# Hybrid MLA and mLSTM step on one core: loops in place of written-out copies, and another split of x over its three tiles

## The chip, the cores and the metric

The kernel runs on one core of one Trainium2 chip. The metric is the device time of one execution in microseconds. The profile is that of one execution; its span runs from the first to the last instruction.

## The reference

One inference step of one layer, on 16 meta tokens, 256 prompt frames and 32 sample frames (304 tokens, `NT`). All projections are column blocks of one matrix `w_in` (4096 by 12,360); everything is float32.

```python
h = rmsnorm(x)                        # x: 304 tokens x 4096
cq, ckv, kpe, mq, mk, mv, mo, mi, mf, za, zb = split(h @ w_in)
q  = rmsnorm(cq) @ w_q_up             # 1536 -> 16 heads x (128 + 64)
kv = ckv_all @ w_kv_up                # 512 -> 16 heads x (128 + 128)
attn = softmax(mask(q k^T)) v         # block-causal over chunks of 64
ml_h = mlstm(mq, mk, mv, mi, mf)      # 4 heads, q and k 256 wide, v 512 wide
y = x + concat(attn * silu(za), sigmoid(mo) * rmsnorm(ml_h) * silu(zb)) @ w_out
```

## The kernel before

Each engine has its program of its own, and semaphores order them. A weight matrix goes through in units of 128 rows by 512 columns (384 or 512 in the attention stage). For each unit SyncE loads float32 rows into `raw` (4 slots of two units), ACT casts a unit to `whi` (L490, type fp32r), DVE subtracts and stores the remainder `wlo` (L857), and TensorE multiplies with both: the helper `mm3` does hi*hi (L1297), lo*hi (L1300) and hi*lo (L1301). `whi` and `wlo` have 4 slots (`HL_SLOTS`). ACT's and DVE's programs run 3 units ahead of TensorE's (`AHEAD`): the helper `steps` prepares unit k + 3 at step k, where the last three steps of a group prepare the first three units of the next. ACT waits for `unit_used` from TensorE, DVE for `hi_done` from ACT, TensorE for `lo_done` from DVE, and SyncE for `lo_done` too.

A group is 512 columns over all 32 units (`group` on TensorE): 32 x 12 matmuls into four PSUM banks, then four evictions, two by ACT and two by DVE. The stages are: x (below); `cq`, 3 groups; `ckv` and `narrow`; `bulk0` and seven `step` phases, each of which runs the projection of one pair of heads (12 units of `w_q_up`, 4 of `w_kv_up`) with the attention of the pair before placed between its units by hooks; `ml0qk`, `ml0v` and three `ml` phases, each with two groups and the mLSTM of one head in hooks; `gate0`, ten groups as five `gates` phases of two, `gate11`; `out0` and seven `out` groups of `w_out`. On TensorE, ACT and DVE all of this is written out by Python's `for`: the program is straight. SyncE and POOL have loops with a register (`Fori`) at the same places; SyncE's loop over the four mLSTM heads is at L416, and its loads are at L374.

The start: x is loaded in rows into three tiles `xt[0..2]` of 128 partitions by 4096, whose numbers of rows `X_TOK` gives: 112, 96, 96. All six DMAs are issued by ACT, first `xt[2]` (64 prompt rows, 32 sample rows), then `xt[0]` (16 meta rows, 96 prompt rows), then `xt[1]` in two halves of 2048 columns. ACT squares and sums each tile (L513, and L501 and L505 for the halves of `xt[1]`), DVE scales it (L870), and TensorE transposes it column block by column block (`x_tile`, L1323, three transposes for each of 32 blocks, after a wait at L1322 for every eighth block), interleaved with the first group of `cq`. SyncE waits for both halves of `xt[1]` (L383) before it issues the first weights. POOL loads the constants `con` and the gains `Grows`. Transposed, x is `xhi` and `xlo`, 304 columns.

With a Python number a wait's value is a constant; with a loop's variable it is computed in a register. Two places ask which it is: TensorE's `q_units` waits for `cq_lo` only where its pair is a Python number,

```python
                    pe.wait_ge(lo_done, U_PAIR + n * PAIR_UNITS + k + 1)
                    if isinstance(n, int):
                        pe.wait_ge(cq_lo, k + 1)
```

and ACT's first exponential skips a wait for pair 0.

Of the kernel before, what the change touches and what calls it, by code (L numbers as in the profile page):

```python
# [8 lines left out]
SEQ, DEC, PAST, N_META = 256, 32, 128, 16  # L9
# [29 lines left out]
TAIL = C_SAMPLE - 256  # L39

X_TOK = [(0, 112), (112, 96), (208, 96)]

WIDE = 72
# [16 lines left out]
XH = (slice(0, D_MODEL // 2), slice(D_MODEL // 2, D_MODEL))  # L62
# [105 lines left out]
def hymba_step(nc, x_prompt, x_sample, cache_ckv, cache_kpe, state_C, state_n, state_m, meta, norm_gain,  # L168
# [8 lines left out]
    with ctx:  # L177
        def keep(stack):
            return lambda name, shape, dt=f32: stack.enter_context(nc.sbuf_tensor(name, shape, dt))

        def sem(name):
            return ctx.enter_context(nc.semaphore(name))
# [27 lines left out]
        xt = [keep(p1)(f"xt{t}", [P, D_MODEL]) for t in range(3)]  # L210
# [113 lines left out]
        xrow_in = [sem(f"xrow{t}_in") for t in (0, "1_left", 2, "1_right")]  # L324
# [136 lines left out]
        def steps(n, now, after, hooks=lambda k: None):  # L461

            for k in range(n):
                if k + AHEAD < n:
                    now(k + AHEAD)
                elif after is not None:
                    after(k + AHEAD - n)
                hooks(k)
# [2 lines left out]
        @block.scalar  # L472
        def _(act):
            nc.scalar.preload_act_table_set("natural_log_exp_and_others")
            act.dma_start(xt[2][0:64, :], x_prompt[0, 192:256, :]).then_inc(xrow_in[2], 16)
            act.dma_start(xt[2][64:96, :], x_sample[0, :, :]).then_inc(xrow_in[2], 16)
            act.dma_start(xt[0][0:N_META, :], meta).then_inc(xrow_in[0], 16)
            act.dma_start(xt[0][N_META:112, :], x_prompt[0, 0:96, :]).then_inc(xrow_in[0], 16)
            for half, t in enumerate((1, 3)):
                act.dma_start(xt[1][0:96, XH[half]], x_prompt[0, 96:192, XH[half]]).then_inc(xrow_in[t], 16)  # L480
            junk = attnT[:, :, :].rearrange("p a b -> p (a b)")

            def unit(u, local, t, width=512):
# [12 lines left out]
            for done, t in enumerate(X_ORDER):  # L496
                n = X_TOK[t][1]
                if t == 1:
# [22 lines left out]
            def cq_units(i):  # L521
                return lambda k: unit(i * KT + k, k, landed(T_CQ, k, i * turns))
# [12 lines left out]
            def cq_evict(i):  # L535

                for ct in (0, 2):
                    act.wait_ge(full[ct], use("cq", ct, 0, i) + 1)
                    nc.scalar.copy(cqraw[:, ds(i * 4 + ct, 1), :], bank[ct][:, 0:NQ]).then_inc(free[ct], 1)
# [4 lines left out]
                    cq_units(0)(AHEAD - 1)  # L544
            steps(KT, cq_units(0), cq_units(1), lambda k: x_tile(k + 4) if k + 4 < KT else None)
            cq_evict(0)
            for i in range(1, 3):
                steps(KT, cq_units(i), cq_units(i + 1))
                cq_evict(i)

# [16 lines left out]
            def pair_units(n):  # L567
                def split(k):
                    unit(U_PAIR + n * PAIR_UNITS + k, k, landed(T_PAIR, k, n * pair_turns), 384 if k < KQ else 512)
                return split  # L570
# [36 lines left out]
            def v_evict(phase, i, n):  # L607

                for half, b in ((0, 1), (1, 2)):
                    act.wait_ge(full[b], use(phase, b, 1, i) + 1)  # L610
                    nc.scalar.copy(vt[:, 2 * half:2 * half + 2, :], bank[b][:, :].rearrange("p (a c) -> p a c", a=2))\  # L611
                      .then_inc(free[b], 1)
# [50 lines left out]
            def attention(phase, i, j):  # L663
                def hooks(k):
                    if k == 1:
                        k_rstd(phase, i, j)
                    if k == 6:
                        exps(phase, i, j, 0)
                    if k == 10:
                        pt_main(phase, i, j, 0)  # L670
                        exps(phase, i, j, 1)
                    if k == 12:
                        attn_evict(phase, i, j, 0)
                        pt_main(phase, i, j, 1)
                    if k == 13:
                        attn_evict(phase, i, j, 1)
                    if k == 15 and phase == "step":
                        q_rstd(phase, i, j + 1)
                return hooks
# [2 lines left out]
                return lambda k: unit(u + k, k, landed(before, k, extra, dmas))  # L682

            act.wait_ge(prob_zero, 1)
            for j in range(0, 6):
                steps(PAIR_UNITS, pair_units(j + 1), pair_units(j + 2), attention("step", j, j))
                v_evict("step", j, j + 1)
            steps(PAIR_UNITS, pair_units(7), big_units(U_ML, T_ML, 0, 2), attention("step", 6, 6))
# [85 lines left out]
                                      Cout[:, 0:2, :]).then_inc(Cp_out, 16)  # L774
                return hooks

            for h in range(0, 3):
                qk = big_units(U_ML + 2 * KT + h * (2 * KT), T_ML, (h + 1) * (3 * turns), 2)
                v = big_units(U_ML + 3 * KT + h * (2 * KT), T_ML, (h + 1) * (3 * turns) + 2 * turns)
                steps(KT, qk, v, mlstm("ml", h, h))  # L780
                qk_evict("ml", h, h + 1)

                steps(KT, v, big_units(U_ML + 4 * KT + h * (2 * KT), T_ML, (h + 2) * (3 * turns), 2))
                mv_evict("ml", 1, h, h + 1)
                act.wait_ge(Cp_out, 16 * h + 16)
# [12 lines left out]

            steps(KT, gate_units(0), gate_units(1), mlstm("gate0", 0, 3))
            gate("gate0", 0, 0)  # L800
            for g in range(0, 5):
                steps(KT, gate_units(2 * g + 1), gate_units(2 * g + 2))
                gate("gates", g, 2 * g + 1, 4)
                steps(KT, gate_units(2 * g + 2), gate_units(2 * g + 3))
                gate("gates", g, 2 * g + 2)
# [32 lines left out]
                    nc.scalar.copy(yT[:, ct, :], bank[ct][:, 0:NQ]).then_inc(free[ct], 1)  # L838

            y_evict("out0", 0, 0)  # L840
            for g in range(0, 6):
                steps(KT, out_units(g + 1), out_units(g + 2))
                y_evict("out", g, g + 1)
            steps(KT, out_units(7), None)
# [4 lines left out]
        def _(dve):  # L849
# [10 lines left out]
            for done, t in enumerate(X_ORDER):  # L860
                n = X_TOK[t][1]
                if done == 2:
# [27 lines left out]
                    cq_units(0)(k)  # L890
            steps(KT, cq_units(0), cq_units(1), lambda k: x_tile(k + 4) if k + 4 < KT else None)
            cq_evict(0)
            for i in range(1, 3):
                steps(KT, cq_units(i), cq_units(i + 1))
                cq_evict(i)

# [164 lines left out]
            def big_units(u):  # L1061
                return lambda k: unit(u + k, k)

            for j in range(0, 6):
                steps(PAIR_UNITS, pair_units(j + 1), pair_units(j + 2), attention("step", j, j))
                pair_end(j, j + 1)
            steps(PAIR_UNITS, pair_units(7), big_units(U_ML), attention("step", 6, 6))
# [148 lines left out]
                            ALU.mult, ALU.add).then_inc(free[7], 1)  # L1216
                return hooks

            for h in range(0, 3):
                qk = big_units(U_ML + 2 * KT + h * (2 * KT))  # L1220
                v = big_units(U_ML + 3 * KT + h * (2 * KT))
                steps(KT, qk, v, mlstm("ml", h, h))
                qk_evict("ml", h, h + 1)
                steps(KT, v, big_units(U_ML + 4 * KT + h * (2 * KT)))
                mv_evict("ml", 1, h, h + 1)
                dve.wait_ge(Cs_out, 16 * h + 16)
# [6 lines left out]

            steps(KT, big_units(U_GATE), big_units(U_GATE + KT), mlstm("gate0", 0, 3))
            silu("gate0", 0, 0)
            for g in range(0, 5):
                odd, even, after = (big_units(U_GATE + n * KT + g * (2 * KT)) for n in (1, 2, 3))
                steps(KT, odd, even)
                silu("gates", g, 2 * g + 1, 4)
                steps(KT, even, after)  # L1240
                silu("gates", g, 2 * g + 2)
# [35 lines left out]
                        add_rows("out", g, g)  # L1277
                return hooks

            for g in range(0, 6):  # L1280
                steps(KT, big_units(U_OUT + KT + g * KT), big_units(U_OUT + 2 * KT + g * KT), out_hooks(g))
                y_evict("out", g, g + 1)
                dve.wait_ge(y_out, g * 48 + 48)
# [8 lines left out]
        def _(pe):  # L1292
# [24 lines left out]
            def x_tile(k):  # L1317
                b = 4 + k % 4
                fill("x", b, k // 4)
                for t, (c0, n) in enumerate(X_TOK):  # L1320
                    if t == 0 and k % (KT // X_PARTS) == 0:
# [29 lines left out]
            for k in range(4):  # L1351
                x_tile(k)
            group(0, "cq", 0, 0, N_META, lambda k: x_tile(k + 4) if k + 4 < KT else None, x_ready=True)
            for i in range(1, 3):
                group(i * KT, "cq", 0, i, N_META)

            def cq_squares(k):
# [214 lines left out]
            pe.wait_ge(qn_zero, 1)  # L1572
            pe.wait_ge(prob_zero, 1)
            pe.wait_ge(pt_zero, 1)
            for j in range(0, 7):
                q_units(j + 1, "step", j, attention("step", j, j))
                kv_units(j + 1, "step", j, attention("step", j, j))
            group(U_ML, "ml0qk", 0, 0, 0, attention("ml0qk", 0, 7), queries=2)
# [138 lines left out]
                    pe.wait_ge(free[b], use("ml0v", b) + 1 + 2 * h)  # L1717

            pe.wait_ge(ml_zero, 6)
            for h in range(0, 3):  # L1720
                group(U_ML + 2 * KT + h * (2 * KT), "ml", 0, h, 0, mlstm("ml", h, h), queries=2)
                group(U_ML + 3 * KT + h * (2 * KT), "ml", 1, h, 0)
            group(U_GATE, "gate0", 0, 0, N_META, mlstm("gate0", 0, 3))

            for g in range(0, 5):
                group(U_GATE + KT + g * (2 * KT), "gates", 0, g, N_META, b0=4)
                group(U_GATE + 2 * KT + g * (2 * KT), "gates", 0, g, N_META)

# [16 lines left out]
                        ins = tr(bank[b][0:m, ct * P:ct * P + P], yT[:, ct, q0:q0 + m], ident)  # L1745
                    ins.then_inc(full[b], 1)

            for g in range(0, 7):
                group(U_OUT + KT + g * KT, "out", 0, g, N_META,
                      lambda k: y_rows("out", g) if k == 2 else None, a_hi=mhi, a_lo=mlo)  # L1750
            y_rows("outlast", 0)
# [234 lines left out]
```

## Time and profile before

| | |
|---|---|
| median of 3 runs | 2138.62 us (2138.28 to 2139.48) |
| the profiled execution | 2138.62 us |
| its span | 2137.0 us |
| TensorE busy, matmuls | 2089.4 us, 98% of the span |
| DVE, ACT, POOL busy | 49%, 42%, 10% |
| granted clock of TensorE, mean | 0.997 |

The profiled execution's time is 1.6 us longer than its span. PE is TensorE's matmul, PEld its weight load; a busy share is an average over all stages. A wait is listed under the engine that waited and the one that ended it.

### The profile page before, as it was taken

The page shows a single profiled execution, that of the slowest core. Times are in us where ns is not written, and L with a number is a line of the kernel's source. Part 1 is how long each engine was busy: PE and PEld are TensorE (multiplying, and loading weights), DVE is VectorE, ACT ScalarE, POOL GpSimd, SP SyncE. Part 2 cuts the span into 40 slices and gives each one's busy share as a digit, 9 for nine tenths or more (in the row PEclk, how much of TensorE's full clock was granted, in tenths as well). Part 3 has the DMA queues.
Part 4 walks back from the last instruction along what each step waited for, and adds up shares of the span by engine and source line. Part 5 has one row for each costly group of instructions (what it writes and reads, how often), then busy time and mean ns, then how long its engine had stood idle before and what let it go on. Part 6 is the DMA issues. An engine that isn't in the chain of part 4 may idle for free.

```text
span 2137.0 us, 38018 instructions
## 1 busy us (share of the span) xinstructions
PE 2089.4 (98%) x15062; PEld 2029.1 (95%) x15062; DVE 1047.2 (49%) x1868; ACT 891.4 (42%) x1751; POOL 218.5 (10%) x292
## 2 busy tenths in 40 slices
PE   4999999999999999999999999999999999999997
PEld 3999999999999899998999999999999999999997
DVE  4544565655544444443444444444445654444443
ACT  4543454545443333343333444444444543333332
POOL 1000123333200000000000000000001100000000
PEclk9999999999999999999999999999999999999999
DMA  7555433232455454554545555555555555555553
GB/s 195 155 164 159 117 121 94 89 104 80 119 149 163 119 163 122 153 145 118 178 123 155 167 167 164 165 167 167 165 163 166 164 181 183 180 180 183 186 188 105
DMA packets 189984, 321.92 MB, mean 151 GB/s; under 512 B 20524, under 2 KB 65680, under 8 KB 189424
## 3 DMA queue, kind: packets, MB, share of 16 engines
q1 hardware_dynamic: 182464, 296.92, 47.0%
q0 software_dynamic: 5488, 15.11, 2.1%
q10 hardware_dynamic: 1872, 7.60, 1.4%
q8 instruction: 119, 1.95, 0.4%
q14 instruction: 41, 0.34, 0.1%
HBM read 309.96 MB, written 9.62 MB: 150 GB/s over the span
## 4 chain that ended last, share of the span: by engine, by line
PE 97%; DMA 1%; DVE 0%; ACT 0%; issue 0%; ACTq 0%; POOL 0%; POOLq 0%; DVEq 0%; SPq 0%
PE bank L1297 29%; PE bank L1301 28%; PE bank L1300 28%; DMA xt<-in_x_prompt_dram 1%; PE bank L1693 1%; PE bank L1656 1%; PE bank L1545 1%; PE bank L1442 1%; PE bank L1443 1%; PE bank L1440 1%; PE bank L1457 1%; PE bank L1499 1%; PE bank L1510 1%; PE bank L1511 1%; PE bank L1745 0%; PE bank L1323 0%
## 5 line engine op out<-in xcount | busy, mean ns | idle before, releaser
L857 DVE TENSOR_TENSOR wlo<-raw,whi 128x512 fp32r<-128x512 f32 (+1 forms) x1256 | 824.3, 665 | 987.3 <-ACT whi L490 984.1
L490 ACT CAST whi<-raw 128x512 fp32r<-128x512 f32 (+1 forms) x1256 | 713.0, 577 | 1085.4 <-PE bank L1301 1043.9
L1297 PE MATMUL bank<-xhi,whi 128*128 128x288 f32 (+2 forms) x3104 | 936.7, 302 | 1.5 <-DVE wlo L857 1.2
L1301 PE MATMUL bank<-xhi,wlo 128*128 128x288 f32 (+2 forms) x3104 | 925.3, 298 | 0.0
L1300 PE MATMUL bank<-xlo,whi 128*128 128x288 f32 (+2 forms) x3104 | 924.2, 298 | 0.0
L1297 PEld LDWEIGHTS bank<-xhi,whi 128*128 128x128 f32 (+1 forms) x3104 | 585.0, 188 | 5.2 <-DVE wlo L857 1.5
L1300 PEld LDWEIGHTS bank<-xlo,whi 128*128 128x128 f32 (+1 forms) x3104 | 585.4, 189 | 1.9 <-issue 1.1
L1301 PEld LDWEIGHTS bank<-xhi,wlo 128*128 128x128 f32 (+1 forms) x3104 | 584.1, 188 | 0.0
L1297 PE MATMUL bank<-mhi,whi 128*128 128x288 f32 x1024 | 304.0, 297 | 0.0
L1300 PE MATMUL bank<-mlo,whi 128*128 128x288 f32 x1024 | 302.5, 295 | 0.0
L1301 PE MATMUL bank<-mhi,wlo 128*128 128x288 f32 x1024 | 302.5, 295 | 0.0
L1297 PEld LDWEIGHTS bank<-mhi,whi 128*128 128x128 f32 x1024 | 193.2, 189 | 0.9
L1300 PEld LDWEIGHTS bank<-mlo,whi 128*128 128x128 f32 x1024 | 193.1, 189 | 0.0
L1301 PEld LDWEIGHTS bank<-mhi,wlo 128*128 128x128 f32 x1024 | 192.7, 188 | 0.0
L1297 PE MATMUL bank<-cqhi,whi 128*128 128x288 f32 x288 | 92.1, 320 | 1.3 <-ACT vt L611 0.7
L1301 PE MATMUL bank<-cqhi,wlo 128*128 128x288 f32 x288 | 85.0, 295 | 0.0
L1300 PE MATMUL bank<-cqlo,whi 128*128 128x288 f32 x288 | 84.8, 295 | 0.0
L1297 PEld LDWEIGHTS bank<-cqhi,whi 128*128 128x128 f32 x288 | 54.4, 189 | 5.2 <-DVE wlo L857 1.1
L1300 PEld LDWEIGHTS bank<-cqlo,whi 128*128 128x128 f32 x288 | 54.6, 189 | 1.3 <-issue 1.2
L1301 PEld LDWEIGHTS bank<-cqhi,wlo 128*128 128x128 f32 x288 | 54.4, 189 | 0.0
L1943 POOL DMA_DIRECT2D out_dram<-ytok x24 | 12.9, 540 | 391.2 <-DVE ytok L1270 388.4
L1850 POOL TENSOR_SCALAR prob<-prob,pinv 128x144 f32<-128x144 f32 (+2 forms) x48 | 40.7, 862 | 116.6 <-DVE pinv L1028 116.6
(314 smaller groups left out, 1377.5 us busy)
## 6 DMA issues: line engine op xcount, KB each, us to landing
raw<-in_w_in_dram SPq DMA_DIRECT2D x316, 512.0 KB, 3.8
raw<-in_w_out_dram SPq DMA_DIRECT2D x128, 512.0 KB, 3.7
raw<-in_w_in_dram SPq DMA_DIRECT2D x140, 256.0 KB, 2.9
raw<-in_w_q_up_dram SPq DMA_DIRECT2D x48, 384.0 KB, 3.3
raw<-in_w_kv_up_dram SPq DMA_DIRECT2D x16, 512.0 KB, 3.7
xres<-in_x_prompt_dram POOLq DMA_DIRECT2D x16, 256.0 KB, 4.9
out_dram<-ytok POOLq DMA_DIRECT2D x16, 256.0 KB, 3.1
C<-in_state_C_dram POOLq DMA_DIRECT2D x4, 512.0 KB, 5.1
```

The source lines that it names most:

```text
L490: ins = nc.scalar.copy(hi, src)
L857: ins = tt(lo, src, hi.bitcast(f32), ALU.subtract)
L1297: ins = mm(out, w_hi, m_hi, start=start, stop=False, **kw)
L1300: mm(out, w_hi, m_lo, start=False, stop=False, **kw)
L1301: return mm(out, w_lo, m_hi, start=False, stop=stop, **kw)
L1440: mm(out, ckhi[:, k, cs], vcols(whi), start=k == 0 and half == 0, stop=False, skip_group_check=True)
L1442: mm(out, cklo[:, k, cs], vcols(whi), start=False, stop=False, skip_group_check=True)
L1443: ins = mm(out, ckhi[:, k, cs], vcols(wlo), start=False, stop=last, skip_group_check=True)
L1457: mm(bank[b][:, 0:NQ], ones if t < 2 else blockones, sq3[:, t, :], start=True, stop=True)\
L1499: mm(bank[b][:, 0:NKV], ones, sq2[:, t, :], start=True, stop=True).then_inc(full[b], 1)
L1510: mm(out, qn[:, h, q0:q0 + P], kn[:, h, 0:keys], start=True, stop=False)
L1850: ts_(prob[0:n, at:at + w], prob[0:n, at:at + w], pinv[0:n, t:t + 1], None, ALU.mult).then_inc(pn, 1)
```

## The change

`X_TOK` becomes 104, 100, 100, and the DMAs of x follow it. Ten `for` loops on ACT and DVE (five each) and five on TensorE become `Fori` loops with a register of the engine: `cq` groups 1 and 2, the `step` pairs (0 to 5 on ACT and DVE, 0 to 6 on TensorE), the `ml` heads 0 to 2, the `gates` phases 0 to 4, and the `out` groups (0 to 5 on ACT and DVE, 0 to 6 on TensorE). Their bodies are the same text. The diff, with one of each kind of loop in full and the rest cut:

```diff
-X_TOK = [(0, 112), (112, 96), (208, 96)]
+X_TOK = [(0, 104), (104, 100), (204, 100)]
...
-            act.dma_start(xt[2][0:64, :], x_prompt[0, 192:256, :]).then_inc(xrow_in[2], 16)
-            act.dma_start(xt[2][64:96, :], x_sample[0, :, :]).then_inc(xrow_in[2], 16)
+            act.dma_start(xt[2][0:68, :], x_prompt[0, 188:256, :]).then_inc(xrow_in[2], 16)
+            act.dma_start(xt[2][68:100, :], x_sample[0, :, :]).then_inc(xrow_in[2], 16)
             act.dma_start(xt[0][0:N_META, :], meta).then_inc(xrow_in[0], 16)
-            act.dma_start(xt[0][N_META:112, :], x_prompt[0, 0:96, :]).then_inc(xrow_in[0], 16)
+            act.dma_start(xt[0][N_META:104, :], x_prompt[0, 0:88, :]).then_inc(xrow_in[0], 16)
             for half, t in enumerate((1, 3)):
-                act.dma_start(xt[1][0:96, XH[half]], x_prompt[0, 96:192, XH[half]]).then_inc(xrow_in[t], 16)
+                act.dma_start(xt[1][0:100, XH[half]], x_prompt[0, 88:188, XH[half]]).then_inc(xrow_in[t], 16)
...
-            for i in range(1, 3):
+            with act.Fori(1, 3) as i:
                 steps(KT, cq_units(i), cq_units(i + 1))
                 cq_evict(i)
...
-            for j in range(0, 6):
+            with dve.Fori(0, 6) as j:
                 steps(PAIR_UNITS, pair_units(j + 1), pair_units(j + 2), attention("step", j, j))
                 pair_end(j, j + 1)
...
-            for h in range(0, 3):
+            with pe.Fori(0, 3) as h:
                 group(U_ML + 2 * KT + h * (2 * KT), "ml", 0, h, 0, mlstm("ml", h, h), queries=2)
                 group(U_ML + 3 * KT + h * (2 * KT), "ml", 1, h, 0)
...
-            for g in range(0, 5):
+            with pe.Fori(0, 5) as g:
                 group(U_GATE + KT + g * (2 * KT), "gates", 0, g, N_META, b0=4)
                 group(U_GATE + 2 * KT + g * (2 * KT), "gates", 0, g, N_META)
...
-            for g in range(0, 7):
+            with pe.Fori(0, 7) as g:
                 group(U_OUT + KT + g * KT, "out", 0, g, N_META,
                       lambda k: y_rows("out", g) if k == 2 else None, a_hi=mhi, a_lo=mlo)
```

## Rows read from the trace of the kernel before

**Rows 1.** The page: busy time, share and instructions of each engine.

```profile
PE 2089.4 (98%) x15062; PEld 2029.1 (95%) x15062; DVE 1047.2 (49%) x1868; ACT 891.4 (42%) x1751; POOL 218.5 (10%) x292
```

**Rows 2.** Stretches: length, busy us (count) by engine, clock, DMA share, GB/s.

```profile
0.00:34.40 34.40, 2.65 (x13) 2.17 (x13) 8.92 (x12) 16.81 (x21) 7.80 (x19) 1.00 0.89 212
2119.00:2137.00 18.00, 5.34 (x41) 4.82 (x40) 2.79 (x5) 0.80 (x2) 1.61 (x3) 0.81 0.09 33
```

**Rows 3.** Stretches of one cq group, step, ml, gates and out phase.

```profile
146.10:197.30 51.20, 51.20 (x387) 51.09 (x386) 22.95 (x35) 20.53 (x34) 0.00 (x0) 1.00 0.58 165
355.90:392.50 36.60, 36.60 (x250) 34.26 (x250) 21.25 (x55) 18.76 (x58) 12.00 (x14) 1.00 0.29 93
688.74:818.85 130.11, 130.11 (x877) 121.40 (x877) 55.91 (x103) 47.27 (x86) 2.94 (x4) 0.99 0.48 142
1290.00:1392.20 102.20, 102.20 (x772) 102.20 (x772) 49.93 (x73) 42.06 (x72) 8.02 (x8) 1.00 0.58 166
1760.79:1813.21 52.42, 52.42 (x398) 52.26 (x397) 24.58 (x37) 20.55 (x34) 3.23 (x6) 1.00 0.56 183
```

**Rows 4.** The chain of waits, its head: start us, us, what.

```profile
3.91 23.54 DMA xt<-in_x_prompt_dram
...
27.53 4.13 DMA raw<-in_w_in_dram
...
34.46 0.61 PE bank L1297
```

**Rows 5.** The stretch of that DMA of x.

```profile
3.91:27.45 23.54, 0.00 (x0) 0.00 (x0) 4.70 (x2) 10.31 (x10) 5.23 (x11) 1.00 1.00 223
```

**Rows 6.** DMA issues of x: count, KB each, median us to landing.

```profile
xt<-in_x_prompt_dram ACTq DMA_DIRECT2D x1, 1536.0 KB, 17.9
xt<-in_x_prompt_dram ACTq DMA_DIRECT2D x2, 768.0 KB, 21.8
xt<-in_x_prompt_dram ACTq DMA_DIRECT2D x1, 1024.0 KB, 7.8
```

**Rows 7.** SyncE's instructions by source line, 663.1:793.1, then 662.5:664 us.

```profile
L374 SPq FUSED_REGOPS  x48: 37/37/51, 665.6 to 792.3; - x48
L374 SPq MOVE raw<-in_w_in_dram x48: 29/29/29, 665.7 to 792.4; - x48
L374 SPq DMA_DIRECT2D raw<-in_w_in_dram x48: 372/373/986, 665.7 to 792.5; - x48
...
L373 SPq FUSED_REGOPS  x31: 46/51/51, 666.7 to 789.5; - x31
...
L416 SPq COMPARE_BRANCH  x1: 45/45/45, 662.9 to 662.9; - x1
L416 SPq FUSED_REGOPS  x1: 68/68/68, 663.2 to 663.2; - x1
```

**Rows 8.** TensorE by source line: the wait, and its transposes.

```profile
L1322 PEldq EVENT_SEMAPHORE  x1: 51/51/51, 42.9 to 42.9; - x1
...
L1323 PEld LDWEIGHTS bank<-con,xt x3: 142/142/142, 45.0 to 45.3; 96*128 96x128 f32 x2, 112*128 112x128 f32 x1
```

**Rows 9.** DMA queues (packets, MB, share of 16 engines) and small issues.

```profile
q8 instruction: 119, 1.95, 0.4%
q14 instruction: 41, 0.34, 0.1%
...
qpm<-in_barred_keys_dram POOLq DMA_DIRECT2D x2, 3.4 KB, 2.8
...
out_dram<-mrow POOLq DMA_DIRECT2D x2, 0.0 KB, 2.0
```

**Rows 10.** Timeline at two boundaries: start us, us, engine, line.

```profile
95.15 0.40 ACT L539 COPY attnT<-bank 128x288 f32<-128x288 f32 x1 [0.21 <-PE bank L1301]
...
95.28 0.81 DVE L885 COPY attnT<-bank 128x288 f32<-128x288 f32 x2
...
380.40 2.14 DVE L989 SCALAR_TENSOR_TENSOR qn<-qn,gsc,rsb 128x288 f32<-128x288 f32 x2
```

More of the change, by code:

```diff
@@ L684, in _ @@
             act.wait_ge(prob_zero, 1)
-            for j in range(0, 6):
+            with act.Fori(0, 6) as j:
                 steps(PAIR_UNITS, pair_units(j + 1), pair_units(j + 2), attention("step", j, j))
@@ L775, in mlstm @@
                 return hooks
-            for h in range(0, 3):
+            with act.Fori(0, 3) as h:
                 qk = big_units(U_ML + 2 * KT + h * (2 * KT), T_ML, (h + 1) * (3 * turns), 2)
@@ L800, in _ @@
             gate("gate0", 0, 0)
-            for g in range(0, 5):
+            with act.Fori(0, 5) as g:
                 steps(KT, gate_units(2 * g + 1), gate_units(2 * g + 2))
@@ L840, in _ @@
             y_evict("out0", 0, 0)
-            for g in range(0, 6):
+            with act.Fori(0, 6) as g:
                 steps(KT, out_units(g + 1), out_units(g + 2))
@@ L892, in _ @@
             cq_evict(0)
-            for i in range(1, 3):
+            with dve.Fori(1, 3) as i:
                 steps(KT, cq_units(i), cq_units(i + 1))
@@ L1062, in big_units @@
                 return lambda k: unit(u + k, k)
-            for j in range(0, 6):
+            with dve.Fori(0, 6) as j:
                 steps(PAIR_UNITS, pair_units(j + 1), pair_units(j + 2), attention("step", j, j))
@@ L1217, in mlstm @@
                 return hooks
-            for h in range(0, 3):
+            with dve.Fori(0, 3) as h:
                 qk = big_units(U_ML + 2 * KT + h * (2 * KT))
@@ L1235, in _ @@
             silu("gate0", 0, 0)
-            for g in range(0, 5):
+            with dve.Fori(0, 5) as g:
                 odd, even, after = (big_units(U_GATE + n * KT + g * (2 * KT)) for n in (1, 2, 3))
@@ L1278, in out_hooks @@
                 return hooks
-            for g in range(0, 6):
+            with dve.Fori(0, 6) as g:
                 steps(KT, big_units(U_OUT + KT + g * KT), big_units(U_OUT + 2 * KT + g * KT), out_hooks(g))
@@ L1353, in _ @@
             group(0, "cq", 0, 0, N_META, lambda k: x_tile(k + 4) if k + 4 < KT else None, x_ready=True)
-            for i in range(1, 3):
+            with pe.Fori(1, 3) as i:
                 group(i * KT, "cq", 0, i, N_META)
@@ L1574, in _ @@
             pe.wait_ge(pt_zero, 1)
-            for j in range(0, 7):
+            with pe.Fori(0, 7) as j:
                 q_units(j + 1, "step", j, attention("step", j, j))
@@ L1719, in _ @@
             pe.wait_ge(ml_zero, 6)
-            for h in range(0, 3):
+            with pe.Fori(0, 3) as h:
                 group(U_ML + 2 * KT + h * (2 * KT), "ml", 0, h, 0, mlstm("ml", h, h), queries=2)
@@ L1723, in _ @@
             group(U_GATE, "gate0", 0, 0, N_META, mlstm("gate0", 0, 3))
-            for g in range(0, 5):
+            with pe.Fori(0, 5) as g:
                 group(U_GATE + KT + g * (2 * KT), "gates", 0, g, N_META, b0=4)
```

## The prediction

> **What bounds the kernel now.** I read the busy times, then the table by stretches, then the head of the chain of waits. TensorE executes 15062 pairs of a weight load and a matmul and is busy 2089.4 of 2137.0 us [rows 1]. Its idle time is 47.6 us: 34.40 - 2.65 = 31.8 us ahead of the first real matmul and 18.00 - 5.34 = 12.7 us at the end [rows 2], so only some 3 us between. The reader is to see that after 34.4 us nothing but TensorE sets the pace, a pair every 0.13 us (51.20 / 387) [rows 3], and that work on another engine costs nothing while it is not late for it. Ahead of 34.4 us the chain is the loading of x: its transfers end at 3.91 + 23.54 = 27.45 us, then SyncE's first weights take 4.13 us, and TensorE starts at 34.46 us [rows 4]. In that stretch all 16 DMA engines are busy, share 1.00 at 223 GB/s [rows 5]. The profiled execution took 2138.62 us, which is also the median of the runs; its 1.6 us over the span stay. A difference under 0.2% (4.3 us) can't be told from none.
>
> **Part 1: the split of x.** No row is added: still 304 rows of 16 KB. The transposes keep their count (three a tile) and together their 304 columns; the squares and scalings of ACT and DVE run over the same 4096 elements, on 100 or 104 partitions: cost 0. What changes is how many rows one DMA carries. Before: 64, 32, 16, 96 and twice 96 half rows, with the sizes in [rows 6], all multiples of 16, so that each engine gets 4 + 2 + 1 + 6 + 3 + 3 = 19 rows. After: 68, 32, 16, 88, and twice 100 half rows. Sixteen engines can't share these equally, and no DMA of before from ACT or SyncE shows how such a one is dealt. The bounds:
>
> - as evenly as whole rows allow: the busiest engine gets 5 + 2 + 1 + 6 + 3.5 + 3.5 = 21, two more. At 23.54 / 19 = 1.24 us a row [rows 4] that is +2.5 us, and 0 if the others' lead is of use.
> - equal shares over as many engines as divide the rows: 68 over 4, 88 over 11, 100 over 10, each time from the same engine on. The first four get 17 + 2 + 1 + 8 + 5 + 5 = 38 rows, the last five 3. The pace then lies between 1.24 us and that of an uncrowded engine: 183 GB/s at share 0.56 [rows 3] is 20.4 GB/s an engine, 0.80 us a row. 38 rows take 30.4 to 47.1 us in place of 23.5: +6.9 to +23.6 us.
>
> I take the second deal, because equal shares are all that the transfers of before have. For the pace I take 0.90 us, near the uncrowded end, since eleven engines carry the bulk at first and four at the end: 38 x 0.90 - 23.5 = +10.7 us. The last half of xt[1] gates the last square and, through SyncE's wait, every weight transfer queued behind it; so all of it moves TensorE's start one for one, and nothing covers it. The Trainium skill (DMA: Bandwidth & Descriptors, "Why a DMA increments its semaphore by 16 and not by 1") states such a rule: the largest number of engines up to 16 that divides the slowest dimension, 10 for 100 partitions, and the lowest-numbered ones for DMAs from ACT or SP. By that rule 68 rows go to 4 engines; no row of before tests it.
>
> **Part 2: loops in place of written-out copies.** The same matmuls, casts and subtractions run. Added are a register instruction for each wait whose value depends on the loop's variable, and a branch an iteration. SyncE has such loops already: there a register instruction takes 0.04 to 0.07 us, and after a branch the next begins 0.3 us later [rows 7]. On TensorE one such wait a unit is 0.05 us against 12 x 0.13 = 1.6 us. Its sequencer has room: the wait at L1322 is over at 42.9 us, the transposes that it belongs to begin at 45.0 us [rows 8], so it works 2.1 us ahead. ACT and DVE are idle half the time [rows 1]. Cost 0; bounds -0.5, for the `cq_lo` waits that seven pairs lose, and +3, if 24 iterations lose 0.12 us each.
>
> The price is in fetching code. TensorE's queue fetched 119 packets of 16.4 KB, one for every 253 instructions, each taking 0.004 x 16 x 2137 / 119 = 1.15 us [rows 1, 9]; code that runs straight on is fetched ahead and shows no wait. A branch back may find its target gone. A fetch then costs between the 2.0 us of the smallest store and 2.8 + 1.15 = 4.0 us, a small load's landing and the packet [rows 9]; I take 3.0, and 0.3 for the branch. Of this 2.1 us are hidden by work already queued, which leaves 1.2 us each (0.2 to 2.2). TensorE branches back 1 + 6 + 2 + 4 + 6 = 19 times (cq, step, ml, gates, out). How many pay, no row says. The nearest is SyncE's loop over the heads: 3 x 48 + 31 + 3 = 178 instructions, more than one packet of its kind (8.3 KB, some 128), and it goes on after 0.3 us [rows 7, 9]; so more than the current packet is kept. TensorE's bodies fill 2 packets (step, 500 instructions), 3 (cq and out, some 780), 6 (gates, 1544) and 7 (ml, 1754 and its waits) [rows 3]. Between 0 and 19 I take those of gates and ml, 6 x 1.2 = +7.2 us: only these bodies are far from SyncE's in packets. The Trainium skill (Runtime: NRT & Kernel Launch, "Instruction fetch mechanics") is of two minds here: it gives TensorE room for 2048 instructions, by which at most ml would pay, and says that a taken branch out of a window of two pages waits for a fetch, by which nearly all 19 would. The trace has no loop on TensorE and settles neither.
>
> ACT and DVE branch back 17 times each. At the end of a column group of cq ACT's last eviction ends at 95.15 + 0.40 = 95.55 us and DVE's at 95.28 + 0.81 = 96.09 [rows 10]. TensorE then has three prepared units, 4.8 us from 95.8 on; the next needs 0.62 us of cast and 0.69 of subtraction before that. So ACT may lose 3.5 us and DVE 3.7 before TensorE waits: a fetch of 3.0 is hidden. Tightest is a pair's end: DVE is done at 380.40 + 2.14 = 382.54 [rows 10] and the fourth unit is due near 385.1, three units of 9 matmuls (3.6 us) and the squares of k (1.3) after 380.1; less the subtraction the cover is 1.9 us. DVE's body there is short: cost 0, or 5 x 1.4 = 7 us if it fetches. SyncE and POOL only follow.
>
> **The sum.** 2138.6 + 10.7 + 7.2 = **2156.5 us**.
>
> **Rivals.**
> 1. All 19 branches of TensorE fetch: 19 x 1.2 = 22.8; with part 1, 2172. For it: the shortest body already fills two packets, and one more is fetched ahead. Against: SyncE's loop.
> 2. No branch costs anything that shows: 2138.6 + 10.7 = 2149. For it: the 2.1 us ahead, and SyncE's loop. Against: bodies of six and seven packets.
> 3. The rows of x are dealt nearly evenly (+1.2): 2140 with free branches, 2147 with six that pay, 2163 with all. For it: each row can be a packet of its own. Against: that the sizes of before never needed it. The first of the three is no change.
> 4. Faster: the seven pairs of the step loop lose 12 waits each (84) on TensorE, at 0.05 us [rows 8] 4.3 us. It decides where TensorE's sequencer sets the pace there and part 1 costs nothing; 2134. Against it: TensorE is busy 36.60 of 36.60 us of a pair [rows 3].
> 5. As rival 1, with ACT and DVE late as well, or x at the slow end of its pace: 2185.
>
> **How the numbers follow.** Forecast (uneven deal, some branches pay) 0.36; rival 1 0.26; rival 2 0.20; rival 3 0.09, of it 0.05 within 0.2%; rival 4 0.02; rival 5 0.07. Faster 0.02, same 0.05, slower 0.93. The range leaves out rivals 4 and 5, most of rival 3 and the outer ends of the pace of x: 2145 to 2177.
>
> **What would show it.** Part 1: the DMA of x at the head of the chain lasts 34 us in place of 23.5, at a DMA share well under 1.00, and the first real matmul starts near 45 us. Part 2: TensorE is idle about a microsecond at the six boundaries of gates and ml and at none of step, cq and out; its fetched packets stay near 119 if bodies are fetched anew each time, and fall to some 50 if they are kept. Wrong would be: a first matmul before 38 us (the deal), or gaps at all 19 boundaries or at none. A gap that begins with a late subtraction on DVE, not in TensorE's own queue, would put the fault on the cover that I gave ACT and DVE.

## The result, and the profile after

The changed kernel takes 2194.84 us (median, 2193.24 to 2196.82), the kernel before 2139.05 (2138.28 to 2140.36): a ratio of 1.0261, 95% interval 1.0243 to 1.0279, so slower by 2.6%. The forecast was slower, by 18 us, in a range that ended at 2177; the loss is 56 us. The profiled execution took 2192.28 us, its span is 2190.7, 53.7 over that of before. One execution of the kernel before, beside the last experiments, took 2570 us at a mean granted clock of 0.75; no ratio counts it.

The page of the kernel after: busy time of the engines, the two queues that fetch code, and the costliest group of TensorE.

```profile
PE 2102.0 (96%) x15062; PEld 2040.3 (93%) x15062; DVE 1041.0 (48%) x1868; ACT 892.6 (41%) x1751; POOL 214.9 (10%) x292
...
q8 instruction: 104, 1.70, 0.3%
q14 instruction: 27, 0.21, 0.0%
...
L1297 PE MATMUL bank<-xhi,whi 128*128 128x288 f32 (+2 forms) x3104 | 942.0, 303 | 24.4 <-issue 21.8
```

TensorE executes the same 15062 pairs as in [rows 1], and is busy 12.6 us longer for them, so a part of the loss is a slower TensorE and not an idle one. Its idle time is 88.7 us in place of 47.6. The releaser "issue" means that the engine waited for nothing that the profile shows.

The start. The head of the chain of waits after (start us, us, what), TensorE's timeline at its first real matmul, and stretches of the loading of x (length, busy us by engine, clock, DMA share, GB/s):

```profile
3.39 42.29 DMA xt<-in_x_prompt_dram
45.75 4.74 DMA raw<-in_w_in_dram
```
```profile
53.28 0.61 PE L1297 MATMUL bank<-xhi,whi 128*128 128x288 f32 x1 [1.83 <-DVE wlo L857]
```
```profile
3.39:45.68 42.29, 0.39 (x1) 0.18 (x1) 4.80 (x4) 10.30 (x10) 5.74 (x12) 1.00 0.60 131
20.00:28.00 8.00, 0.00 (x0) 0.00 (x0) 0.00 (x0) 0.00 (x0) 0.00 (x0) 1.00 0.65 128
28.00:36.00 8.00, 0.00 (x0) 0.00 (x0) 0.63 (x1) 4.21 (x4) 0.00 (x0) 1.00 0.45 129
36.00:46.00 10.00, 0.39 (x1) 0.18 (x1) 4.28 (x4) 6.40 (x7) 0.00 (x0) 1.00 0.20 80
```

Against [rows 4, 5]: the transfers of x last 42.29 us, not 23.54, and TensorE starts at 53.28, not 34.46: 18.8 us. The share falls step by step, from 16 x 0.65 = 10 engines at work to 16 x 0.20 = 3: engines run out of rows one group after another, and a few work to the end. Equal shares give just that: four engines with 38 rows, six with 21, one with 11 and five with 3.

The loops. The idle time of TensorE by what ended it (total us, times, longest us), then the branches that close its five loops, each by its source line: cq, step, ml, gates, out (duration ns min/median/max, first and last start us):

```profile
PE bank L1315 <- DMA con<-in_shape_table_dram: 40.4, 1, 40.4
PE bank L1297 <- issue: 21.8, 6, 4.7
PE bank L1323 <- DVE xt L870: 8.4, 1, 8.4
```
```profile
L1354 PEldq COMPARE_BRANCH  x2: 83/167/251, 164.1 to 215.2; - x2
...
L1575 PEldq COMPARE_BRANCH  x7: 83/215/227, 360.9 to 581.0; - x7
...
L1720 PEldq COMPARE_BRANCH  x3: 83/4529/4772, 828.0 to 1094.3; - x3
...
L1725 PEldq COMPARE_BRANCH  x5: 76/3696/3793, 1271.3 to 1705.4; - x5
...
L1748 PEldq COMPARE_BRANCH  x7: 76/208/223, 1859.9 to 2174.1; - x7
```

Here the trace says it directly. The last branch of each loop falls through and takes 0.08 us. One that jumps back takes 0.2 us at cq, step and out, but 4.5 and 4.8 at ml and 3.3 to 3.8 at gates. TensorE stands still six times, as often as these two loops jump. First and last start give the iterations: ml (1094.3 - 828.0) / 2 = 133.15 us, gates (1705.4 - 1271.3) / 4 = 108.5, against 130.11 and 102.20 in [rows 3]; cq 51.1, step 36.7 and out 52.4 are as they were. That is 2 x 3.04 + 4 x 6.32 = 31.4 us. Another 1.0 us lies behind the late start: in its first 15.8 us of real matmuls TensorE executes 105, before 113, because those of 0.24 us go on for 5.8 us there and not for 3.0. With the 18.8 us, 51 of the 53.7 are placed; the rest is not.

A gates iteration is 6.3 us longer, but its gap is shorter: the four are 4.67, 3.85, 4.20 and 4.31 us, 4.3 in the mean. TensorE's timeline at the first, and stretches behind it:

```profile
1273.46 0.29 PE L1301 MATMUL bank<-xhi,wlo 128*128 128x288 f32 x1
1278.42 0.61 PE L1297 MATMUL bank<-xhi,whi 128*128 128x288 f32 x1 [4.67 <-issue]
1278.83 0.44 PE L1300 MATMUL bank<-xlo,whi 128*128 128x288 f32 x1
1279.07 0.44 PE L1301 MATMUL bank<-xhi,wlo 128*128 128x288 f32 x1
```
```profile
1278.42:1282.00 3.58, 3.58 (x15) 3.58 (x16) 0.69 (x1) 0.91 (x2) 0.00 (x0) 0.50 0.12 17
1282.00:1286.00 4.00, 4.00 (x24) 4.00 (x24) 1.38 (x2) 0.94 (x2) 0.00 (x0) 0.69 0.39 120
1286.00:1300.00 14.00, 14.00 (x108) 14.00 (x107) 5.95 (x9) 5.58 (x9) 0.00 (x0) 1.00 0.56 152
```

The branch starts at 1271.3, and the queued pairs cover it until 1273.75. After 4.67 us of idle the granted clock is 0.50 (1.2 GHz): 15 matmuls in 3.58 us, 0.24 us each and not 0.13, for some 6 us; behind the second and third gap it is some 3 us. From 1286 on it is back at 2.4 GHz. The remaining 2.1 us of the mean iteration lie there.

### The profile page after: what moved, and what is told of

It reads as the page before. It is cut to its first block, busy times and chain, and to the rows that moved or that the text cites. A ratio compares the mean times of both kernels' runs of the same rounds, so it can differ in the third digit from the quotient of the medians.

```text
span 2190.7 us, 41123 instructions
## 1 busy us (share of the span) xinstructions
PE 2102.0 (96%) x15062; PEld 2040.3 (93%) x15062; DVE 1041.0 (48%) x1868; ACT 892.6 (41%) x1751; POOL 214.9 (10%) x292
## 4 chain that ended last, share of the span: by engine, by line
PE 95%; DMA 2%; issue 1%; DVE 0%; ACT 0%; POOL 0%; ACTq 0%; DVEq 0%; POOLq 0%; SPq 0%
PE bank L1297 28%; PE bank L1300 28%; PE bank L1301 28%; DMA xt<-in_x_prompt_dram 2%; PE bank L1693 1%; PE bank L1656 1%; PE bank L1545 1%; PE bank L1443 1%; PE bank L1442 1%; PE bank L1440 1%; PE bank L1457 1%; PE bank L1499 1%; PE bank L1510 1%; PE bank L1511 1%; PE bank L1745 0%
## 5 line engine op out<-in xcount | busy, mean ns | idle before, releaser
L1297 PE MATMUL bank<-xhi,whi 128*128 128x288 f32 (+2 forms) x3104 | 942.0, 303 | 24.4 <-issue 21.8
```

What stands on the lines that cost most here:

```text
L1297: ins = mm(out, w_hi, m_hi, start=start, stop=False, **kw)
```

## The experiments

Theory of the split: rows are dealt in equal shares, over as many engines as divide them, and the first four engines get 38 of them. Rival: the number of DMAs, other tiles, or a nearly even deal. Theory of the loops: a jump back to code that TensorE no longer keeps waits for a fetch; rivals are late ACT or DVE, the branch itself, and what the bodies hold. "Before" is the kernel before, run on the same chip beside each set.

| kernel | us, median | ratio to before (95%) |
|---|---|---|
| loops only | 2176.94 | 1.0168 (1.0151 to 1.0185) |
| split only | 2158.49 | 1.0078 (1.0061 to 1.0095) |
| split, DMAs of 16 rows and remainders | 2146.93 | 1.0028 (1.0018 to 1.0038) |
| long bodies written out | 2140.79 | 0.9999 (0.9990 to 1.0009) |
| gates head at slot 0 | 2148.78 | 1.0037 (1.0024 to 1.0049) |
| hints at ml and gates | 2145.00 | 1.0018 (1.0009 to 1.0028) |
| out loop of two groups | 2177.04 | 1.0166 (1.0150 to 1.0183) |
| gates head at slot 200 | 2164.70 | 1.0113 (1.0093 to 1.0133) |
| the same with a hint | 2147.61 | 1.0037 (1.0025 to 1.0050) |
| both loops mended | 2141.64 | 1.0005 (0.9996 to 1.0014) |
| tiles 104, 104, 96 | 2148.97 | 1.0043 (1.0028 to 1.0057) |
| ten DMAs, one of 16 rows each time | 2142.91 | 1.0018 (1.0008 to 1.0028) |
| ten DMAs, equal cuts | 2146.36 | 1.0029 (1.0018 to 1.0040) |
| first 64 rows as 62 + 2 | 2163.70 | 1.0113 (1.0091 to 1.0135) |
| the change with both parts mended | 2146.56 | 1.0034 (1.0021 to 1.0047) |

Beside these, before had medians of 2140.3 to 2141.1 us, over a range of 2137.4 to 2143.0. Its profiled start is at the early end too: eight kernels here with its own six DMAs of x start real matmuls at 35.1 to 36.1 us, it at 34.46. Differences of a microsecond at the start, or of two in a median, are noise. The kernel with 62 + 2 rows was executed only twice.

### The parts by themselves

Loops only: the changed kernel with the old `X_TOK` and the old DMAs of x.

> The changed kernel with the split of x of the kernel before; all loops stay. If the two parts add up, the gaps that the profile after shows at the six back-branches of ml and gates stay (2.6 to 2.8 us at ml, 4.1 to 5.0 at gates, iterations longer by 2.9 and by 5 to 7 us), and the start is that of before, first matmul at 34.5 us: about 2139 + 6 + 25 = 2170 us. If the late start had caused the gaps (rival), they are gone and the time is 2139 to 2142.

Split only: the kernel before with the new ones.

> The kernel before with the new split of x alone. The uneven deal of rows over engines gives a DMA of x of some 42 us, a first matmul near 53 us and 2139 + 19 to 22 = 2158 to 2161 us. If the late start came from the loops (rival: code fetched on the same queues), it is 2139.

+35.8 us and +17.4 us: together 53.2, of 55.8 for the whole. The parts add up, and the late start caused no gap. The branches of the loops-only kernel at ml and gates:

```profile
L1720 PEldq COMPARE_BRANCH  x3: 76/4309/4697, 811.1 to 1078.3; - x3
...
L1725 PEldq COMPARE_BRANCH  x5: 76/3816/3886, 1255.3 to 1690.9; - x5
```

Iterations of 133.6 and 108.9 us: 7 + 27 = 34 us of its 35.8; I had expected 31.

### Which loops

Long bodies written out, in the loops-only kernel:

```diff
-            with pe.Fori(0, 3) as h:
+            for h in range(0, 3):
...
-            with pe.Fori(0, 5) as g:
+            for g in range(0, 5):
```

> The loops-only kernel with TensorE's two long loops (ml, gates) written out again; its cq, step and out loops stay, as do all loops of ACT and DVE. If only the long bodies pay, it takes the time of before, 2138 to 2141 us. If the loops of ACT and DVE have a part in the gaps (rival), some of the 31 us stays and shows as waits of TensorE for a subtraction at the ends of iterations of ml and gates: 2145 to 2170.

The time of before, with TensorE's 13 other back-branches and all those of ACT and DVE in place. So the whole loss of the loops comes from six branches.

### Length, or place

Out loop of two groups, in the loops-only kernel:

```diff
-            with pe.Fori(0, 7) as g:
-                group(U_OUT + KT + g * KT, "out", 0, g, N_META, ...
+            with pe.Fori(0, 3) as n:
+                for g in (2 * n, 2 * n + 1):
+                    group(U_OUT + KT + g * KT, "out", 0, g, N_META, ...
+            group(U_OUT + 7 * KT, "out", 0, 6, N_META, ...
```

> The loops-only kernel, with TensorE's out loop as 3 iterations of two column groups (some 1600 instructions a body, as gates has) and the seventh group written out; its loop of one group (some 780) showed no gap at 6 back-branches. If the length of the body decides, 2 gaps of 2.6 to 5 us appear at out and the time is 5 to 14 us over the loops-only kernel, 2175 to 2184. If it is what the bodies hold or where they lie (rival), none appears and it is 2170.

No new gap at out, and the time of the loops-only kernel (2177.04 and 2176.94). The body, 2 x 398 pairs [rows 3] and some 70 others, 1666 recorded instructions, is longer than that of gates and costs nothing, so length alone does not decide:

```profile
L1748 PEldq COMPARE_BRANCH  x3: 83/226/227, 1897.1 to 2106.6; - x3
```

The next kernel moves the gates body without changing it:

```diff
-            with pe.Fori(0, 5) as g:
+            with nc.Fori(0, 5, engines=OrderedEngineSet([pe.engine]), head_slot={pe.engine: 0}) as g:
```

> The loops-only kernel, with the head of TensorE's gates loop put at the start of a packet of code (254 to 256 instructions) by padding; nothing else changes. In the profile after, each back-branch of gates is followed by two packets in a row, some 3.2 us apart, at ml by one. Theory A (the head lies near the end of a packet, so the second packet is needed at once): one fetch is left to wait for, gaps fall from 4.1 to 5.0 us to 1.5 to 2.8 and with less slow clock after them, 2155 to 2163 us. Theory B (a body of that length is kept if it spans no packet more than needed): no gaps at gates at all, only those of ml stay, near 2145. Theory C (neither matters): as the loops-only kernel, 2170.

Theory B held: the gaps of gates are gone. And with `head_slot={pe.engine: 200}`:

> The loops-only kernel with the head of TensorE's gates loop put at slot 200 of a packet of 256 instructions. The body has some 1610 instructions: from slot 0 it ends in the seventh packet, from 200 in the eighth (200 + 1610 = 1810, over 1792). If the body is kept as long as it lies in seven packets, the gaps of 4 to 5 us at four back-branches are back, 27 us of them: 2170 to 2177 us. If the padding alone mended them in the kernel with the head at slot 0 (rival), none: 2149.

They are back, though shorter. TensorE's branches at gates (a placed loop has one more, the jump into its head), its waits on "issue" and its packets of code, first with the head at slot 0 (the idle left is that of ml):

```profile
L1726 PEldq COMPARE_BRANCH  x6: 76/212/295, 1154.0 to 1663.9; - x6
```
```profile
PE bank L1298 <- issue: 6.3, 3, 2.9
```
```profile
q8 instruction: 68, 1.11, 0.2%
```

and at slot 200:

```profile
L1726 PEldq COMPARE_BRANCH  x6: 76/4723/5198, 1149.9 to 1678.8; - x6
```
```profile
PE bank L1298 <- issue: 16.9, 8, 3.0
```
```profile
q8 instruction: 105, 1.72, 0.4%
```

The gates body has 772 pairs [rows 3] and 65 others, 1609 instructions recorded from one closing branch to the next. A packet holds 256: TensorE's 30538 recorded instructions of the kernel before came in 119, 256.6 each. From slot 0 the body ends in the seventh packet, from 200 in the eighth. In seven it is kept, in eight fetched anew at each turn, 37 packets more. The rival that padding alone mends is out.

The total was 5 us under my expectation because the gaps are 2.4 to 3.0 us here, and 3.9 to 4.7 in the changed kernel, although the branch is longer here (4.6 to 5.2 us, against 3.3 to 3.8). The trace of the changed kernel shows what follows its first branch at gates, by source line:

```profile
L1725 PEldq FUSED_REGOPS  x1: 50/50/50, 1275.2 to 1275.2; - x1
L1311 PEldq ALU_OP  x1: 36/36/36, 1275.3 to 1275.3; - x1
```

Two instructions of the body run, and the third, a weight load, starts at 1278.42, 3.1 us later. The fetches of two packets start at 1272.6 and 1275.8 us. So it is at all eight waiting branches of gates in this kernel and the loops-only one: a stop of 2.8 to 3.4 us after two instructions. The head therefore lies two instructions before the end of its packet, at slot 254, and a second fetch is waited for at once. From there the body ends at 254 + 1609 = 1863, over 7 x 256 = 1792: eight packets.

From this head the recorded instructions can be counted to the others of the loops-only kernel and of the one with the out loop of two groups. The ml head is 1855 + 1000 instructions earlier, at slot 215; TensorE does run 256 - 215 = 41 instructions behind a branch at ml and then waits 0.7 and 0.9 us more. The head of the out loop of two groups is 1609 + 1573 later, at slot 108, and its body ends at 108 + 1666 = 1774. That is in the seventh packet, so its 0.2 us follow the same rule.

### The hint

```profile
L1726 PEldq COMPARE_BRANCH  x6: 88/228/292, 1149.6 to 1659.5; - x6
```
```profile
q8 instruction: 69, 1.13, 0.2%
```

Branches of 0.2 us and 36 packets fewer, and none fetched from 1237 to 1661 us: with the hint a body of eight packets is kept. It does not only order the target early. From this I made a rule, seven packets without and eight with a hint, and from it what mends ml, which has more than seven packets of code from any slot. Both loops mended has the gates head at slot 0, and `head_slot={pe.engine: 0}, hint_back_edge=True` on ml:

> The loops-only kernel with the gates head at slot 0 without a hint, and the ml head at slot 0 with a hint. The runs so far fit this rule: without a hint a body is kept if it lies in seven packets (gates from slot 0, the loops of up to 1674 instructions), with one if it lies in eight (gates from slot 200, after which no packet was fetched until the loop ended). The ml body has some 1817 instructions, 25 over seven packets, so it lies in eight from slot 0 and in nine from most other slots. If the rule holds, ml is kept too: no gap at any of the 19 back-branches, no packet fetched for TensorE between 830 and 1050 us, and 2140 to 2143 us, as the kernel with these two loops written out. If the hint only orders the target early (rival), ml's code is fetched anew each time and what it showed with a hint elsewhere stays, 1.6 and 2.3 us an iteration: 2144 to 2146 us.

```profile
L1721 PEldq COMPARE_BRANCH  x4: 80/234/310, 680.6 to 1070.3; - x4
...
L1726 PEldq COMPARE_BRANCH  x6: 76/212/401, 1143.8 to 1653.7; - x6
```
```profile
q8 instruction: 49, 0.80, 0.2%
```

The rule held. No branch of the 19 waits, 49 packets are fetched, and the time can't be told from that of before. One count in my expectation was wrong: the body has 1855 recorded instructions, 1856 with the hint, and touches nine packets only from slots over 192, not from most. In the kernel with hints its head lay in such a slot: again 41 instructions run behind the branch before TensorE waits, so it is slot 215, 215 + 1856 = 2071 is over 8 x 256, and ml paid in spite of its hint (branches of 2.9 and 3.1 us). Slot 0 without a hint was not tried at ml.

### The deal of x

Split with DMAs of a multiple of 16 rows and a remainder:

```diff
-            act.dma_start(xt[2][0:68, :], x_prompt[0, 188:256, :]).then_inc(xrow_in[2], 16)
+            act.dma_start(xt[2][0:64, :], x_prompt[0, 188:252, :]).then_inc(xrow_in[2], 16)
+            act.dma_start(xt[2][64:68, :], x_prompt[0, 252:256, :]).then_inc(xrow_in[2], 16)
...
-                act.dma_start(xt[1][0:100, XH[half]], x_prompt[0, 88:188, XH[half]]).then_inc(xrow_in[t], 16)
+                act.dma_start(xt[1][0:96, XH[half]], x_prompt[0, 88:184, XH[half]]).then_inc(xrow_in[t], 16)
+                act.dma_start(xt[1][96:100, XH[half]], x_prompt[0, 184:188, XH[half]]).then_inc(xrow_in[t], 16)
```

> As the one before it, but each DMA of 68, 88 and 100 rows is cut into one of a multiple of 16 rows (64, 80, 96) and a rest of 4 or 8; the same tiles of 104, 100 and 100 rows. If the deal of rows over engines is the cause, most of the lateness goes: the busiest engines have 4 + 1 + 2 + 1 + 5 + 1 + 3.5 + 3.5 = 21 rows, 2 more than before, so about 2.5 us late, 2141 us. If the tiles' sizes or the count of rows on partitions were the cause (rival), it stays at 2158 to 2161.

Two thirds are back (from +17.4 to +5.8 us), where I expected nearly all. Tiles of 104, 104 and 96 rows, with DMAs of 88 and twice 104 rows as the odd ones:

> The kernel before with x split into tiles of 104, 104 and 96 rows: DMAs of 64, 32, 16, 88 rows and twice 104 half rows. If equal shares over as many engines as divide the rows decide, 64 rows go to 16 engines, 88 to 11, 104 to 13, and the busiest get 4 + 2 + 1 + 8 + 4 + 4 = 23 rows, against 38 in the split of the change and 19 before. At the 1.12 us a row of the split-only kernel (42.44 / 38) to the 1.24 of before that is a DMA of x of 26 to 28.5 us, 2 to 5 us late, 2143 to 2146 us. If any size that isn't a multiple of 16 costs alike (rival), the two halves and the 88 rows bring most of the 17 us of the split-only kernel: 2150 to 2158. If the 7 us that the split with remainders kept come from tiles of other sizes, about 2147.

Between the two theories: +8.5 us, 3 over the top of what the deal gives and one under the rival's foot. Only the next one is sharp. The first DMA of before, 64 rows, as 62 and 2:

```diff
-            act.dma_start(xt[2][0:64, :], x_prompt[0, 192:256, :]).then_inc(xrow_in[2], 16)
+            act.dma_start(xt[2][0:62, :], x_prompt[0, 192:254, :]).then_inc(xrow_in[2], 16)
+            act.dma_start(xt[2][62:64, :], x_prompt[0, 254:256, :]).then_inc(xrow_in[2], 16)
```

> The kernel before, its tiles unchanged, with the first DMA of x, 64 rows, cut into one of 62 rows and one of 2. By equal shares over as many engines as divide the rows, 62 go to 2 engines, 31 each, and these have 31 + 1 + 2 + 1 + 6 + 3 + 3 = 47 rows. With 0.66 us for each of the 28 rows over 19 (79 GB/s at share 0.20 in the stretch 36 to 46 us of the split-only kernel is 24.7 GB/s an engine) the DMA ends 18 us late, with its mean of 1.12 us a row for all 47 it lasts 53 us, 29 late: 2159 to 2170 us. If rows are dealt singly to whichever engine is next (rival), it lasts 24 to 25 us and the time is 2141 to 2143.

The head of its chain, and the stretch to the end of x:

```profile
2.71 42.77 DMA xt<-in_x_prompt_dram
```
```profile
27.45:45.48 18.03, 0.39 (x1) 0.18 (x1) 0.28 (x1) 4.20 (x4) 0.00 (x0) 1.00 0.12 49
```

A share of 0.12 is 1.9 of 16 engines: two work, alone, for 18 us. 49 / 1.92 = 25.5 GB/s each, 0.64 us a row, and 28 rows more than the other engines' 19 take 28 x 0.64 = 18 us. The equal shares are shown, and with them the 38 rows of the change. The load ends 18.0 us later than before and the first matmul starts 23.7 later (58.18 us), because `xt[2]`, whose square ACT takes first, is now the tile that comes last.

What stayed open is why the split with remainders kept 5.8 us. Ten DMAs with the old tiles, 16 rows split off each time (48 + 16, 80 + 16, 80 + 16 twice):

> The kernel before, its tiles of 112, 96 and 96 rows unchanged, with the DMAs of 64, 96 and twice 96 rows each cut into a multiple of 16 and one of 16 rows (48 + 16, 80 + 16, 80 + 16 twice): ten DMAs for x, as in the split with remainders, which stayed 5.8 us over before. If the number of DMAs costs that, this kernel takes about 2147 too, with a DMA of x of some 30 us. If the remainders of 4 and 8 rows, which reach 4 or 8 engines, do (rival), each engine has its 19 rows, the DMA stays at 23.5 to 24.5 us and the time at 2141.

and ten with equal cuts (32 + 32, 48 + 48, 48 + 48 twice):

> As the kernel with ten DMAs for x, which ended them at 32.4 us against 27.5 to 27.8 with six, at share 1.00 but 185 GB/s against 223; here the cuts are equal (32 + 32, 48 + 48, and 48 + 48 twice), so no DMA gives an engine a single row. If the number of DMAs slows the engines, they end near 32.4 again and the time is 2142 to 2144. If small ones of one row an engine do (rival), they end by 29 us: 2141.

The stretch of [rows 5] with remainders, with 16 rows split off, with equal cuts, and with tiles of 104, 104 and 96 rows:

```profile
3.91:27.45 23.54, 0.00 (x0) 0.00 (x0) 2.35 (x1) 4.46 (x5) 5.23 (x11) 1.00 1.01 163
```
```profile
3.91:27.45 23.54, 0.00 (x0) 0.00 (x0) 2.35 (x1) 7.88 (x6) 5.23 (x11) 1.00 1.00 185
```
```profile
3.91:27.45 23.54, 0.00 (x0) 0.00 (x0) 2.35 (x1) 7.28 (x5) 5.26 (x11) 1.00 1.02 169
```
```profile
3.91:27.45 23.54, 0.00 (x0) 0.00 (x0) 2.35 (x1) 6.45 (x5) 5.23 (x11) 1.00 0.91 174
```

With ten DMAs the engines are as full as before, share 1.00 to 1.02, and move 163 to 185 GB/s in place of 223. Equal cuts are no better (2146.36 to 2142.91), so small pieces are not the reason. Nor is it the number of DMAs alone: the last row has six, and there a busy engine moves 174 / (16 x 0.91) = 12.0 GB/s, against 13.9 before and 11.6 and 10.4 with ten evenly dealt. Its DMA of x lasts 31.06 us for the 23 rows of the busiest engine, 1.35 us a row, which is where its 3 us over the deal come from. In this stretch every other deal than that of before had slower engines; why, these runs don't tell.

Last, the whole change with the DMAs of the split with remainders and the loops as in the kernel with both loops mended:

> The whole change with both faults mended: the split into 104, 100 and 100 rows with the DMAs in multiples of 16 and remainders, and all loops, with the gates head at slot 0 and the ml head at slot 0 with a hint. If the parts are independent, its time is that of the split with remainders and free loops, 2146 to 2148 us, with no gap at any back-branch. If the later start or more DMAs disturb the fetches (rival), gaps are back and it takes 2150 or more.

2146.56 us, no branch that waits: all 6 us left are those of the split. The two parts are independent within the noise.

## Why the prediction was wrong

**Direction and mechanisms** were right, that gates pays in part by luck: x dealt in equal shares, 38 rows on four engines; a pay at the six back-branches of ml and gates, none at the other 13; ACT and DVE never late, and SyncE's wait passing the late x on to the first weights. Two terms were sized wrong, and both sizes were too small; these are the steps that failed.

**The term "38 x 0.90 - 23.5 = +10.7"** measured 18.8 us (first matmul) and 17.4 (split only). It is inside its bounds of 6.9 to 23.6. What failed is the pace "near the uncrowded end, since eleven engines carry the bulk at first and four at the end". The trace gives 42.29 / 38 = 1.11 us a row. In the stretch 20 to 28 us only 0.65 of the engines were busy, and yet each moved 128 / (16 x 0.65) = 12.3 GB/s, under the 13.9 of a full one in [rows 5]; the uncrowded pace came only after 36 us (80 / 3.2 = 25 GB/s, 0.66 us a row). Fewer busy engines did not make the others faster while ten of them worked, and in that stretch of the loading no kernel with a changed deal kept the pace of before. For bounds so far apart the middle, 1.0 us, would have given 14.5.

**The term "6 x 1.2 = +7.2"** measured 31.4 us, 5.2 a branch, outside its bound of 2.2. The six gaps are 21.8 us of it. It had three faults:

- "A fetch then costs between 2.0 and 4.0 us; I take 3.0". The waiting branch takes 3.3 to 5.2 us over the kernels without hints. Those of ml in the changed kernel, 4.5 and 4.8, leave gaps of 2.3 and 2.5 where 2.2 was the bound. A small load's landing and a packet were no upper bound.
- One fetch was counted a branch. At gates of the changed kernel two are waited for, and the idle time is 3.9 to 4.7 us; with the head at slot 200 and one fetch it is 2.4 to 3.0.
- The clock was left out. Behind the gaps of gates TensorE runs at 0.50 for 3 to 6 us, 2.1 us more an iteration. A stall of the engine that bounds a kernel costs more than itself.

**Which bodies pay.** "Only these bodies are far from SyncE's in packets" picked the right six, but length was not the measure. What decides is the number of packets that the body touches, seven or eight, and that hangs on where its head falls: the same gates body costs nothing at slot 0, and the longer out body nothing at slot 108. The counts of six and seven packets took pairs alone; with the other instructions and the heads at slots 254 and 215 it is eight and nine. ml would pay at any slot without a hint by this rule, but gates only from the 72 slots over 183 of 256. There the layout decided, and the prediction had no reason for it; from the other slots rival 2's free branches would have been true of gates.

**The marks given.** DMA of x 34 us: it took 42.3. First matmul near 45: 53.3. Idle about 1 us at six boundaries: at those six, 2.3 to 4.7. Packets near 119 if fetched anew, some 50 if kept: 104, and 49 once all are kept. Rival 5, 2185, came nearest in time, for reasons that did not hold.

**The pages.** The Trainium skill (DMA: Bandwidth & Descriptors, "Why a DMA increments its semaphore by 16 and not by 1") gives the largest number of engines up to 16 that divides the rows, from the lowest on. The runs agree: two engines for 62 rows, +23 us. The Trainium skill (Runtime: NRT & Kernel Launch, "Instruction fetch mechanics") gives TensorE room for 2048 instructions, and the runs agree, with the qualification that the eighth packet is there only with a hint. Its other statement, that a branch out of a window of two pages waits, differs from the measurement: the out body of two groups, some 1670 instructions, jumps back in 0.2 us. The measurement decides.

## What to carry to other kernels

Before a written-out body becomes a loop, count its instructions in packets of code and ask where the head will lie: the duration of the closing branch in the trace (0.2 us, or 3 to 5) tells in one row whether the body is kept, and a hint or another slot can mend it without a change of the work. Count the rows of a DMA by their divisors, not their sum: 4 rows more than 64 cost 13 more on the busiest engine. Where bounds of a price lie three times apart, and the engine that would wait is the one that bounds the kernel, take the middle or above, and add what the slow clock takes after the stall.

## What was not expected of the hardware

- TensorE keeps a body that touches seven packets (1792 instructions), and eight with a hint at its top: 105 fetched packets against 69 for the same code at the same slot, but for the hint.
- A branch back to code that is gone takes 3.3 to 5.2 us without a hint. A head two instructions before the end of its packet costs a second wait of some 3 us. Behind gaps of 3.9 to 4.7 us half the clock follows for 3 to 6 us.
- Ten DMAs for the same rows, evenly dealt, kept all 16 engines busy at 169 to 185 GB/s where six moved 223; six for other tiles moved 174 at share 0.91.
